# Token copies first, rotary key rows swapped by DMA, key norms summed by rows, and a reordered VectorE in a float32 model block on Trainium2

## The reference, cut to what matters

```python
def first_block(...):
    x = x + einsum(g_a * y_a + g_b * y_b, w_o)
    h = rmsnorm(x, g_ffn)
    u = h @ w_up
    f = gelu(causal_dwconv(u[..., :D_FF], conv_f_w) + conv_f_b) * u[..., D_FF:]
    x = x + f @ w_down
    ...
def _mla_qkv(u, ...):           # 4 heads of 128 plain + 64 rotary features
    q = (_rms(cq) @ w_uq); kv = (_rms(ckv) @ w_ukv)
    k = concatenate([k_nope, broadcast(k_rope)])
    q, k = _rms(q, q_norm_g), _rms(k, k_norm_g)
    # rotary: x * cos + rotate_half(x) * sin, by halves of 32 rows
def _attend(q, k, v):           # 1024 queries, 1280 keys (256 context)
    p = softmax(q k^T * scale); return p v
out = x + gate * (branches @ w_out)
```

## Time and profile before

| | us |
|---|---|
| median of 3 runs (lowest to highest) | 1948.41 (1947.28 to 1950.55) |
| the profiled execution, its own time | 1946.56 |
| its span in the profile | 1943.6 |
| PE busy, share of the span | 1894.9, 97% |
| VectorE / ScalarE / POOL busy | 1391.4 / 711.4 / 906.7 |
| PE in the chain that ended last | 82% (VectorE 11%, ScalarE 3%) |

### The profile page before, as it was taken

The page is one execution under the profiler, slowest core; times in us unless marked ns, Lnnn a source line. Parts: engine busy times, 40 slices in busy tenths (PEclk is TensorE's granted clock), DMA queues, the critical chain, the costliest instruction groups (busy, mean ns, idle before and its releaser), DMA issues.

```text
span 1943.6 us, 24288 instructions
## 1 busy us (share of the span) xinstructions
PE 1894.9 (97%) x9047; PEld 1575.3 (81%) x9047; DVE 1391.4 (72%) x1425; ACT 711.4 (37%) x970; POOL 906.7 (47%) x634
## 2 busy tenths in 40 slices
PE   7999999999998999999999999999999999999998
PEld 6788888778886888888888788878787878888877
DVE  7989988567438989889888785664723756666583
ACT  5433343431234333333330200353321245565543
POOL 6866666533333565555665555423133513212442
PEclk9999999999999999999999999999999999999999
DMA  5122234454112222323265334111141310000052
GB/s 168 44 62 69 87 109 141 143 186 137 44 44 66 87 87 75 97 65 97 65 230 175 127 122 168 44 44 33 33 135 53 89 35 1 12 12 1 1 173 65
DMA packets 190889, 166.40 MB, mean 86 GB/s; under 512 B 11267, under 2 KB 168912, under 8 KB 190800
## 3 DMA queue, kind: packets, MB, share of 16 engines
q1 hardware_dynamic: 189520, 162.82, 26.5%
q10 hardware_dynamic: 1280, 2.35, 0.3%
HBM read 134.73 MB, written 30.41 MB: 85 GB/s over the span
## 4 chain that ended last, share of the span: by engine, by line
PE 82%; DVE 11%; ACT 3%; issue 2%; POOL 1%; DMA 0%; ACTq 0%; DVEq 0%; POOLq 0%
PE ps L953 33%; PE ps L1251 19%; PE ps L1108 15%; PE ps L1665 2%; PE ps L1483 2%; PE ps L1516 1%; PE ps L1518 1%; PE ps L1517 1%; PE ps L1494 1%; PE ps L1500 1%; PE ps L1497 1%; PE ps L1491 1%; PE ps L1503 1%; DVE win_a L2944 1%; DVE prob L2992 1%
## 5 line engine op out<-in xcount | busy, mean ns | idle before, releaser
L824 POOL TENSOR_TENSOR small<-ones 128x1 f32<-128x1 f32 x76 | 25.6, 336 | 501.0 <-PE ps L953 433.1
L953 PE MATMUL ps<-xb_hi,whi 128*128 128x512 f32 x752 | 246.2, 395 | 12.1 <-DVE t L2648 7.0
L953 PE MATMUL ps<-xb_lo,whi 128*128 128x512 f32 x752 | 242.7, 390 | 0.0
L953 PE MATMUL ps<-xb_hi,wlo 128*128 128x512 f32 x752 | 242.5, 390 | 0.0
L829 POOL TENSOR_TENSOR wlo<-raw,whi 128x1024 fp32r<-128x1024 f32 (+1 forms) x73 | 199.0, 2726 | 6.1
L953 PEld LDWEIGHTS ps<-xb_hi,whi 128*128 128x128 f32 x752 | 140.3, 189 | 45.9 <-DVE t L2648 7.4
L869 POOL TENSOR_TENSOR wlo<-w_sums,whi 128x512 fp32r<-128x512 f32 x80 | 137.3, 1735 | 83.1 <-ACT whi L1969 83.1
L953 PEld LDWEIGHTS ps<-xb_lo,whi 128*128 128x128 f32 x752 | 141.5, 188 | 29.9 <-issue 0.2
L953 PEld LDWEIGHTS ps<-xb_hi,wlo 128*128 128x128 f32 x752 | 141.5, 188 | 29.9
L2372 DVE SCALAR_TENSOR_TENSOR ps<-glu_pad,tab,ps 128x1024 f32<-128x1024 f32 x116 | 149.2, 1287 | 2.9
L923 POOL TENSOR_SCALAR prob<-prob,small 128x512 f32<-128x512 f32 x64 | 50.5, 802 | 190.0 <-DVE small L3001 189.7
(11 more groups left out here) (490 smaller groups left out, 4852.9 us busy)
## 6 DMA issues: line engine op xcount, KB each, us to landing
t<-in_w_mod SPq DMA_DIRECT2D x48, 256.0 KB, 2.9
f_scratch<-t SPq DMA_DIRECT2D x22, 512.0 KB, 2.7
raw<-in_w_down SPq DMA_DIRECT2D x22, 512.0 KB, 4.2
raw<-in_w_up SPq DMA_DIRECT2D x40, 256.0 KB, 3.7
w_raw<-in_w_up SPq DMA_DIRECT2D x40, 256.0 KB, 3.7
raw<-in_w_in SPq DMA_DIRECT2D x18, 512.0 KB, 4.0
raw<-in_w_in SPq DMA_DIRECT2D x36, 256.0 KB, 3.9
w_in_raw<-in_w_in SPq DMA_DIRECT2D x32, 256.0 KB, 3.7
```

The costliest lines, as they stand in the source:

```text
L824: nc.gpsimd.tensor_tensor(small[:, 106 + slab.slot:107 + slab.slot], ones[:, 0:1], ones[:, 0:1], ALU.mult)
L953: ins = mm(dst[j], w, r[j], start=first and f, stop=last and l)
```

## The change

- ScalarE makes the 16 token copies ahead of the inverse root.
- The rotation matrix, its load and its product go. Four DMAs, issued by ScalarE, copy the rotary key rows to `U3` with their 16-row groups swapped, and the sine table carries the sign. `rope_in` is now awaited at 96 and 112.
- The rotary squares are kept as high and low parts in `KSQ` (64 rows each); the sums by tokens at the gate tile go. Per head, `key_sums` multiplies them by ones in the rounded type (`onesr`) and the plain squares, which now lie in `rkbc`, by ones in float32, into banks 5 to 7: the sum stands on every partition. ScalarE takes Ln and Exp(-x/2) of it; roots, reciprocals, key scales and their copies go.
- The last value product of the head before lies in bank 2. The values use banks 3, 4, 2, 5, 6; the fourth waits for both Ln. Odd heads' first scores wait for `o_read`.
- ScalarE takes the second query tile's high part ahead of the first Square; VectorE's order changes, and the products of a head's first maxima stand ahead of the query's reciprocal.
- `out_add(0, 1)` stands ahead of the weight sums.

```diff
@@ -282,10 +281,12 @@
     Vl = at("v_lo", [P, KT, 2 * VD], F32R, o_xbh + 43008)
-    sqk = at("sq_head", [P, NKEY], F32, o_xbh + 53248)
+    sqk = at("sq_head", [P, S], F32, o_xbh + 53248)
     PTh = at("pt_hi", [P, KT, 2 * P], F32R, o_xah)
+    KSQ = at("k_rope_squares", [P, NKEY], F32R, o_t + 20480)
+    onesr = at("ones_r", [P, P], F32R, o_t + 25600)
@@ -486,6 +487,10 @@
+    def value_bank(i):
+        b = (3, 4, 2, 5, 6)[i]
+        return PS[:, H * b:H * (b + 1)]
...
@@ -1375,13 +1380,6 @@
-        def key_sums(n):
-            if n == 4:
-                pe.wait_ge(sem("lora_sq"), 4)
-                for t in range(KT):
-                    mm(PS[:, SC + 32 + t:SC + 33 + t], sqkr[:, t * P:(t + 1) * P], ones[0:ROPE, 0:1], start=True, stop=True)
@@ -1396,13 +1394,8 @@
         j, L = Lin(JOBS["ga"]), Lin(SLABS["ga"])
-        gemm(j, L, XBh, XBl, KD, w8, between=key_sums)
+        gemm(j, L, XBh, XBl, KD, w8)
         gemm(j + 1, L + 1, XBh, XBl, KD, w8, between=lora_sums)
-        pe.wait_ge(*free(J + 3))
-        pe.wait_ge(sem("y_ready"), 8)
-        for a in (0, H):
-            last = mm(PS[0:ROPE, ST + a:ST + a + H], rotm[:, :], krT[:, a:a + H], start=True, stop=True)
-        last.then_inc(sem("rot_pe"), 1)
@@ -1431,9 +1424,18 @@
-        def key_sum(t):
-            return mm(PS[:, SC + 256 + t:SC + 257 + t], sqk[:, t * P:(t + 1) * P], ones[:, 0:1], start=True, stop=True)
+        def key_sums(h):
+            if h == 0:
+                pe.wait_ge(sem("ksq_ready"), 2)
+            else:
+                pe.wait_ge(sem("pt_lo"), 6 * 4 * h)
+            for a, b in ((S, NKEY), (0, H), (H, S)):
+                o = PS[:, 5 * H + a:5 * H + b]
+                mm(o, onesr[:, :], KSQ[:, a:b], start=True, stop=False)
+                last = mm(o, ones[:, :], rkbc[:, a:b], start=False, stop=True)
+                if a != 0:
+                    last.then_inc(sem("ksum_pe"), 1)
...
@@ -1459,15 +1451,8 @@
                 mm(o, whi[:, slot, w], CQh[:, k, q], start=k == 0, stop=False)
-                if sums is not None:
-                    key_sum(sums + 2 * k)
                 mm(o, whi[:, slot, w], CQl[:, k, q], start=False, stop=False)
-                if sums is not None:
-                    key_sum(sums + 2 * k + 1)
                 last = mm(o, wlo[:, slot, w], CQh[:, k, q], start=False, stop=k == 1)
-            if sums == 4:
-                key_sum(8)
-                key_sum(9).then_inc(sem("ksum_pe"), 1)
@@ -1549,12 +1534,13 @@
                     turn(before, 5)
-                query_product(h, c, 0, 0, 4 * c).then_inc(sem("nope_pe"), 1)
+                query_product(h, c, 0, 0).then_inc(sem("nope_pe"), 1)
             if h:
-                pe.wait_ge(sem("qr_f"), GOES_ON["qr_f"][1] + h + 1)
-                pv(before, 4 * H)
+                pe.wait_ge(sem("kn_lo"), GOES_ON["kn_lo"][1] + 3 * h + 3)
+                pv(before, 2 * H)
                 warm(2)
+            key_sums(h)
@@ -1562,9 +1548,11 @@
                         pe.wait_ge(sem("o_read"), 4 * h)
+                    if i == 3:
+                        pe.wait_ge(sem("k_log"), 2 * h + 2)
                         keys = slice(k * P, (k + 1) * P)
-                        o = PS[:, H * (2 + i) + 2 * P * (k % 2):H * (2 + i) + 2 * P * (k % 2 + 1)]
+                        o = value_bank(i)[:, 2 * P * (k % 2):2 * P * (k % 2 + 1)]
@@ -1578,19 +1566,13 @@
                 pe.wait_ge(sem("v_lo"), 5 * (h // 2) + 3)
+            elif h:
+                pe.wait_ge(sem("o_read"), g)
             scores(g, 1, 0, 256)
-            pe.wait_ge(sem("k_rcp"), h + 1)
-            if h % 2 == 0:
-                pe.wait_ge(sem("v_lo"), 5 * (h // 2 + 1))
-            if h:
-                pe.wait_ge(sem("pt_lo"), 6 * g)
-                pe.wait_ge(sem("o_read"), g)
-            key_scales(h, 0)
             pe.wait_ge(sem("q_fold"), GOES_ON["q_fold"][1] + 2 * h + 1)
+            pe.wait_ge(sem("k_log"), 2 * h + 1)
             scores(g, 0, 0, 512, 0)
-            key_scales(h, 1)
-            key_scales(h, 2)
...
@@ -1941,8 +1922,8 @@
         act.wait_ge(sem("x2_ready"), 9)
+        token_combs(range(0, KD))
         inverse_root(rbc, D, 2).then_inc(sem("rbc_ready"), 1)
-        token_combs(range(0, KD))
@@ -2093,11 +2074,18 @@
         rope_out(J + 3, 0, S)
+        act.wait_ge(*free(J + 3))
+        for half in (0, 32):
+            for u in range(2):
+                act.dma_start(U3[half + 16 * u:half + 16 * (u + 1), 0:S],
+                              krT[half + 16 * (1 - u):half + 16 * (2 - u), 0:S]).then_inc(sem("rope_in"), 16)
             fn(cqT[:, k, :], pair(j), ACT.Copy).then_inc(*one(free(j)))
+        act.wait_ge(sem("lora_sq"), 4)
+        fn(KSQ[0:ROPE, :], sqkr[:, :], ACT.Copy).then_inc(sem("ksq_hi"), 1)
@@ -2172,7 +2160,7 @@
                 act.wait_ge(sem("kn_lo"), GOES_ON["kn_lo"][1] + 3 * h + c + 1)
-                fn(sqk[:, k], PS[:, k], ACT.Square).then_inc(sem("kn_sq"), 1)
+                fn(rkbc[:, k], PS[:, k], ACT.Square).then_inc(sem("kn_sq"), 1)
@@ -2187,27 +2175,33 @@
                 pool_high(7)
+            fn(sd[:, 12:13], ones[:, 0:1], ACT.Ln)
+            act.wait_ge(sem("nope_pe"), 2 * h + 2)
+            fn(QNh[:, H:S], PS[:, H:S], ACT.Copy, scale=col("q_norm_g_2", 0)).then_inc(sem("qn_hi"), 1)
             fn(sqk[:, 0:H], PS[:, 0:H], ACT.Square).then_inc(sem("qn_sq"), 1)
-            act.wait_ge(sem("nope_pe"), 2 * h + 2)
-            fn(QNh[:, H:S], PS[:, H:S], ACT.Copy, scale=col("q_norm_g_2", 0)).then_inc(sem("qn_hi"), 1)
             fn(QRs[0:ROPE, :], qwork[0:ROPE, :], ACT.Copy).then_inc(sem("qr_hi"), 1)
-            act.wait_ge(sem("k_var"), h + 1)
-            fn(ksd, kvar, ACT.Sqrt, scale=1.0 / QH, bias=eps_col).then_inc(sem("k_sd"), 1)
             fn(sqk[:, H:S], PS[:, H:S], ACT.Square).then_inc(sem("qn_sq"), 1)
+            def value_hi(i):
+                act.wait_ge(sem("v_pe"), 5 * (h // 2) + i + 1)
+                fn(Vh[:, 2 * i:2 * i + 2, :], value_bank(i).rearrange("p (t n) -> p t n", t=2),
+                   ACT.Copy).then_inc(sem("v_hi"), 1)
+            for n, (a, b) in enumerate(((S, NKEY), (0, S))):
+                act.wait_ge(sem("ksum_pe"), 2 * h + n + 1)
+                fn(rkbc[:, a:b], PS[:, 5 * H + a:5 * H + b], ACT.Ln, scale=1.0 / QH, bias=eps_col).then_inc(sem("k_log"), 1)
             if h % 2 == 0:
-                for i in range(KT // 2):
-                    act.wait_ge(sem("v_pe"), 5 * (h // 2) + i + 1)
-                    fn(Vh[:, 2 * i:2 * i + 2, :], PS[:, H * (2 + i):H * (3 + i)].rearrange("p (t n) -> p t n", t=2),
-                       ACT.Copy).then_inc(sem("v_hi"), 1)
-            for j, (k0, k1) in enumerate(((0, 4), (4, 8), (8, 10))):
-                act.wait_ge(sem("kbc"), 3 * h + j + 1)
-                if h and j == 0:
-                    act.wait_ge(sem("s_read"), 8 * h)
-                o = H * (5 + j % 2)
-                fn(rkbc[:, k0 * P:k1 * P], PS[:, o:o + (k1 - k0) * P], ACT.Copy).then_inc(sem("kbc_read"), 1)
+                for i in range(3):
+                    value_hi(i)
+            act.wait_ge(sem("k_log"), 2 * h + 2)
+            fn(rkbc[:, :], rkbc[:, :], ACT.Exp, scale=-0.5).then_inc(sem("k_scale"), 1)
+            if h % 2 == 0:
+                for i in range(3, 5):
+                    value_hi(i)
+            fn(sd[:, 12:13], ones[:, 0:1], ACT.Sqrt)
...
@@ -2907,7 +2901,9 @@
         dve.wait_ge(sem("cols_pe"), 2)
-        link(nc.vector.tensor_copy(krc, PS[:, SC + 32:SC + 32 + KT]))
+        nc.vector.tensor_copy(onesr[:, :], ones[:, :]).then_inc(sem("ksq_ready"), 1)
+        dve.wait_ge(sem("ksq_hi"), 1)
+        tt(KSQ[ROPE:P, :], sqkr[:, :], f32(KSQ[0:ROPE, :]), ALU.subtract).then_inc(sem("ksq_ready"), 1)
@@ -2915,9 +2911,8 @@
         dve.wait_ge(*free(J + 3))
-        dve.wait_ge(sem("rope_in"), 32)
-        dve.wait_ge(sem("rot_pe"), 1)
-        tt(U3[0:ROPE, 0:S], PS[0:ROPE, ST:ST + S], sinb[:, :], ALU.mult).then_inc(sem("krot_mul"), 1)
+        dve.wait_ge(sem("rope_in"), 96)
+        tt(U3[0:ROPE, 0:S], U3[0:ROPE, 0:S], sinb[:, :], ALU.mult).then_inc(sem("krot_mul"), 1)
@@ -2985,13 +2980,19 @@
         def maxima(g, a):
-            t = 2 * (g % 4) + a
+            products(g, a)
+            bias(g, a)
+        def products(g, a):
                                            accum_out=mx[:, a:a + 1]).then_inc(sem("s_read"), 1)
+        def bias(g, a):
+            t = 2 * (g % 4) + a
@@ -3004,7 +3005,7 @@
             part = ga[:, h, :].rearrange("p (q t) -> p t q", t=8)[:, 2 * p:2 * p + 2, :]
-            o = 4 * H if p == 3 and h < HEADS - 1 else SC
+            o = 2 * H if p == 3 and h < HEADS - 1 else SC
@@ -3037,37 +3038,37 @@
             if h == 0:
-                dve.wait_ge(sem("rope_in"), 48)
+                dve.wait_ge(sem("rope_in"), 112)
                 tt(KRl[0:ROPE, :], krot[:, :], f32(KRs[0:ROPE, :]), ALU.subtract).then_inc(sem("kr_lo"), 1)
-            dve.wait_ge(sem("qr_sq"), GOES_ON["qr_sq"][1] + h + 1)
```

(30 more changed lines are left out.)

31 lines of the change are left out of this document (8 added, 23 removed).

## The result

| | before | after |
|---|---|---|
| median of the runs compared | 1948.57 us (4 runs, 1947.28 to 1950.55) | 1923.93 us (4 runs, 1921.07 to 1926.95) |
| profiled execution | 1946.56 us | 1922.31 us |
| its span | 1943.6 us | 1920.4 us |
| mean granted clock | 0.994 | 0.997 |

The ratio is 0.9874, 95% interval 0.9857 to 0.989: 24.6 us less. One execution of the kernel before in a later series took 3725.61 us in a slower state and is left out of every figure here.

What follows compares the result with a forecast made beforehand. The prediction took TensorE, busy for 97% of the span, to bound the kernel. Its terms, 8.8 + 4.2 + 4.3 + 1.0 = 18.3 us, off the 1948.4 us median gave 1930.1 us, range 1925 to 1937.

Steps and rivals of the forecast that it cites:

- Part 1: Token copies ahead of the inverse root: gains 8.8 us, 7.0 of first-gate wait and 1.8 of lower clock.
- Part 2: Rotary keys: TensorE loses the rotation product (1.86 us) and ten one-column sums (2.32 us), gaining 4.2 us.
- Part 3: Key norm by rows in the four heads: gains 4.3 us together, 0.5 in head 0, 1.3, 1.2 and 1.3 after.
- Part 4: Output addition ahead of four weight sums: its 1.1 us wait goes, gain 1.0 us, bounds 0 and 1.1.
- The first maxima: In the heads, first maxima no longer wait for the query's root: of 1.3 us, 0.6 stay.
- Head 0: First head: 3.2 us of waits where 2.0 were, 1.7 us of lower clock back, gain 0.5 us.
- Bank 2: Last value product of the head before moves there and stops waiting for the query's rotary sum: 0.45 us saved.
- (b): Rival: heads give all since waits overlap, 5.7 us more, 1924.4 us; chance 0.12.
- (a): Rival: heads give nothing or lose, new waits bringing lower clock in heads 1 to 3: 1934 to 1936 us; chance 0.17.
- (c): Rival: the token copies' gain is taken back in the combinations from 620 on: 1938.9 us; chance 0.05.
- (d): Rival: slower, ScalarE's queue ends last in every head, 6.1 us lost a head: 1958 us; chance 0.03.
- (e): Rival: parts as worked, but an unseen cost of 14 us or more offsets them: within 0.2%; chance 0.03.

Runs made afterwards that it cites:

- b_copies: Kernel before with only the 16 token copies moved ahead of the inverse root: 1938.9 us against 1946.51, ratio 0.9959.
- a_load_late: Changed kernel without the one-element Ln that fetches the logarithm's table early: 1923.68 us, ratio 0.9874.
- b_all_but_norm: Kernel before with token copies first, earlier output addition and rotary rows by DMA, heads and squares' sums as before: 1937.89 us, ratio 0.9957.
- a_product_late: Changed kernel with each head's first scores' product and maximum back behind the query's root: 1925.93 us, ratio 0.9893.
- a_bank4: Changed kernel with each head's last value product back in bank 4 and the values' banks in order 3, 2, 4, 5, 6: 1929.59 us, ratio 0.9903.
- a_add_late: Changed kernel with the first pair's output addition back behind the weight sums: 1928.28 us, ratio 0.9898.
- number 12: Changed kernel with the unused rotation-matrix load kept at the head of ScalarE's queue: 1924.03 us against 1924.94.
- a_folds_first: Changed kernel with VectorE's second fold ahead of value low parts 4 and 5 (even heads), gating ahead of first fold (odd): 1918.21 us, ratio 0.9847.

## Why the prediction was off, point by point

**Part 1, 8.8: right.** 596.46 + 23.62 − 575.85 became one piece of 35.41; 45.95 − 37.13 = 8.8 us, of which 7.0 are the wait and 1.8 the clock. In the profile of after it survives to the end of the feed-forward part (from the row sums to near 1367 before took 799.84 us and after 790.98), in that of b_copies 8.0 of it do, because of the wait near 990; and alone it moves the median by 7.6 (interval 5.3 to 10.7).

**Part 2, 4.2: right in what goes, short by 1.2.** From the row sums to the kr copy after is 13.34 us shorter than before; 8.8 is part 1's. Through the keys' rotary work itself the changed kernel gained 3.0. The missing 1.2 are TensorE's clock, less a small gain that the sum left out. The 96 matmuls behind the one-column sums L1015 took 23.52 us here and 21.93 in a_load_late, the same instructions at a full clock, 1.6 us less; the lower clock is there in ten of the eleven profiles with the new order and, behind its own sums, in b_all_but_norm, which lacks the rotation product too, but not in before and b_copies, which have it. That suggests a price of the change more than chance; it is not shown. Against it stand 0.4 us: the 204 matmuls of this stretch took 46.92 us in before and 46.46 in a_load_late, all at a clock of 1.00. The prediction had a bound of 3.0, but for another reason. The other 1.5 of the 13.34 come from near 1370: from the sixteen products of L1333 (L1338 in after) to the next long piece of matmuls before took 14.84 us and after 13.39. Both fell to the lower clock there, before for longer; a_load_late, at 1.00 throughout, took 12.83. Nothing in the change is known to cause that.

**Part 3, 4.3: this is the step that failed.** The heads gave 2.97 + 2.05 + 1.89 + 2.22 = 9.1 us. By the prediction's own terms:
- *The first maxima.* That "of the 1.3 us ... 0.6 stay" was worked and never added to the heads' sum. Its 0.7 a head would have been too much; a_product_late measures 0.4, 1.6 us in all.
- *The new waits.* Gating in odd heads, 1.0 put down, 0.4 found; the second fold in head 2, 1.4 put down, 0.8 found. That is 1.8 us over heads 1 to 3. With it and the maxima the forecast would have been 2.3, 2.2 and 2.3; the traces have 2.05, 1.89 and 2.22.
- *Head 0.* The three waits were put at 1.1, 0.9 and 1.2 and came at 0.9, 0.8 and 0.6. The lower clock that I expected "after the new waits too" (1.7) did not come, nor in nine others of the eleven profiles with the new order; only a_load_late, whose edit made the wait for the logarithm 2.3 us long, has it in head 0. The profile of before had it, one of the three with the old order (b_copies) did not: 1.6 us of head 0's 2.97 are that clock, as 31.48 against 29.85 shows, and 1.3 the change.
- *Bank 2.* Put at 0.45 a head; it avoids 1.3 to 2.0 (a_bank4). The sum came out right because the prediction took the 1.9 us of TensorE's saving as kept whole, which only this move makes true. As a term by itself it was too small by a factor of three.
- *Four table loads a head, each 1.28 us:* as forecast. Ln and Exp each fetched theirs, and neither shows a drain ahead of it: the Exp's load starts at 1649.67, when the logarithm before it ends.

```profile
1648.54 1.12 ACT L2195 ACTIVATE k_scale_bc<-ps,small 128x1024 f32<-128x1024 f32 x1 [1.56 <-PE ps L1436]
1649.67 1.28 ACT L2200 ACT_TABLE_LOAD   x1
1650.97 1.27 ACT L2200 ACTIVATE k_scale_bc<-k_scale_bc 128x1280 f32<-128x1280 f32 x1
1652.26 1.28 ACT L2204 ACT_TABLE_LOAD   x1
```

**Part 4, 1.0: a true row read as a price.** The trace gives 1.28, but a_add_late shows that the addition is worth 5.0 us in the changed kernel, and the bound of 1.1 was no bound. A wait against a VectorE that is busy without a pause is as long as TensorE is early. In the profile of before TensorE came 1.1 us late, at a lower clock, and VectorE's own work (L3159) took 0.74 us where b_copies has 1.75; that hid two thirds of it.

**The output stage's entry, not in the sum.** 1.08 us, from the last head to the first output product: 65.2 to 65.5 at a full clock, 66.3 to 66.5 at a lower one, whatever the edit. Chance, in after's favour.

**The start, not in the sum.** −1.63 us, with the rotate load the only edit ahead of it, and number 12 clears that. 1.5 of it is the lower clock behind the wait near 377: the sixteen matmuls from 379.33 took 5.41 us, and 3.88 in before.

**The rivals.** (b), heads that give all because waits overlap, 1924.4, had 0.12 and is what came, though not for its reason: of the 4.8 us that were missing in the heads, waits shorter than worked account for 2.7 (1.8, and 0.9 in head 0), the omitted term for 1.6, head 0's clock for 1.6. These overshoot by 1.1 us over four heads, which no run resolves. (a), a lower clock in heads 1 to 3, took an idle stretch of 1 us as its cause. In after none was longer than 0.8 us and the clock stayed at 1.00; a_bank4 has three of 1.7 us in these heads, and it stayed at 1.00 too; and a_load_late has the lower clock in head 2 behind one of 0.77 us. So the length of the wait does not decide it by itself. (c), (d) and (e) are refuted by the columns above. What decided between forecast and (b) was a term that had been worked out and dropped, and a lower clock charged to the new kernel for a wait that, on the evidence of one profile, seemed to bring it.

What stays open: why one of the three profiles with the old order kept the clock in head 0 and two did not; how often the changed order would have it, beyond ten profiles without and one with it; and where the 0.9 us of a_folds_first beyond its waits come from.

## What to carry to other kernels

When work is taken from the bound engine, ask of every wait behind it how long it is if that engine comes sooner by just the amount saved: the wait of the old trace is its length at the old arrival, and here 0.45 us stood for 1.7 and 1.1 for 3.3. Add up the terms from a list at the end, so that none that was worked out is lost. And before the lower clock of one profile goes into a sum, on either side, give it a chance instead of a price; where marks in the trace allow it, read an edit of some tenths of a microsecond from the stretches that repeat, not from the median.
